# Attention's scaled gate: turned by blocks on VectorE and placed through memory

## The reference

```
attn = _sink_window_attend(q, k, v, qpos, kpos, sinks).reshape(B, T, ATTN_WIDTH)
attn = _rmsnorm(attn, attn_g) * jax.nn.silu(g_attn)
```

## Time and profile before

| | us |
|---|---|
| median of 3 runs | 2558.17 |
| the profiled execution | 2546.3 |
| its span, first to last instruction | 2544.5 |
| PE busy in the span | 2493.5 |
| VectorE busy | 1705.2 |
| ScalarE busy | 1113.5 |
| GpSimd busy | 1172.3 |

### The profile page before, as it was taken

One profiled execution on the slowest core, in us unless ns is written; L12 is line 12 of the kernel. 1 busy time (PEld: TensorE's weight loads), 2 busy tenths in 40 slices (PEclk: granted clock), 3 DMA queues, 4 the chain that ended last, 5 costly groups with the idle time before them and its releaser, 6 DMA issues. The chain is left out here.

```text
span 2544.5 us, 55195 instructions
## 1 busy us (share of the span) xinstructions
PE 2493.5 (98%) x20706; PEld 2044.3 (80%) x20706; DVE 1705.2 (67%) x3230; ACT 1113.5 (44%) x2542; POOL 1172.3 (46%) x1119
## 2 busy tenths in 40 slices
PE   8999989999999999999999999899999999999998
PEld 6788868888888788888888788688888887887887
DVE  5777777777676676654557777776777676866343
ACT  4455465555555510133334454555555554112322
POOL 2234315555556611496322443165555555116863
PEclk9999999999999999999999999999999999999999
DMA  5445552011110488765734555510111005877532
GB/s 182 154 172 185 187 186 70 27 43 43 44 38 25 175 288 293 273 216 172 264 123 154 186 179 178 190 35 31 43 43 51 31 33 195 313 270 257 170 135 91
DMA packets 176099, 365.44 MB, mean 144 GB/s; under 512 B 19104, under 2 KB 98464, under 8 KB 170272
## 3 DMA queue, kind: packets, MB, share of 16 engines
q1 hardware_dynamic: 175504, 363.11, 41.6%
q10 hardware_dynamic: 432, 0.08, 0.0%
HBM read 227.14 MB, written 137.89 MB: 143 GB/s over the span
## 5 line engine op out<-in xcount | busy, mean ns | idle before, releaser
L1947 PE MATMUL r_Z<-w_rec_parts,w_rec_xh 128*128 128x512 f32 x1920 | 610.3, 399 | 1.8 <-DVE r_kT L1768 0.9
L1947 PEld LDWEIGHTS r_Z<-w_rec_parts,w_rec_xh 128*128 128x128 f32 x1920 | 347.7, 188 | 71.9 <-issue 3.5
L1947 PE MATMUL r_Z<-w_rec_parts,w_rec_xl 128*128 128x512 f32 x960 | 375.7, 391 | 0.0
L124 PE MATMUL a_Z<-w_attn_high,w_attn_xh 128*128 128x512 f32 (+1 forms) x816 | 302.3, 370 | 11.6 <-DVE w_attn_low L211 9.7
L124 PE MATMUL a_Z<-w_attn_low,w_attn_xh 128*128 128x512 f32 (+1 forms) x816 | 290.6, 356 | 0.0
L124 PE MATMUL a_Z<-w_attn_high,w_attn_xl 128*128 128x512 f32 (+1 forms) x816 | 290.3, 356 | 0.0
L1649 ACT ACTIVATE r_E<-r_E 128x512 f32<-128x512 f32 x230 | 145.3, 632 | 294.6 <-DVE r_E L1805 292.1
L1540 POOL TENSOR_TENSOR r_qE<-r_qT,r_E 128x256 f32<-128x256 f32 x230 | 185.1, 805 | 190.6 <-ACT r_E L1649 115.4
L1947 PEld LDWEIGHTS r_Z<-w_rec_parts,w_rec_xl 128*128 128x128 f32 x960 | 180.2, 188 | 39.7
L1540 POOL TENSOR_TENSOR r_kE<-r_kT,r_E 128x256 f32<-128x256 f32 x230 | 201.2, 875 | 0.0
L124 PEld LDWEIGHTS a_Z<-w_attn_high,w_attn_xh 128*128 128x128 f32 x816 | 154.8, 190 | 39.9 <-issue 19.3
(11 more groups left out here) (338 smaller groups left out, 6409.3 us busy)
## 6 DMA issues: line engine op xcount, KB each, us to landing
dram_h_rows<-o_hb SPq DMA_DIRECT2D x34, 512.0 KB, 4.1
o_raw<-dram_hT SPq DMA_DIRECT2D x34, 512.0 KB, 4.3
o_hb<-dram_h_rows SPq DMA_DIRECT2D x34, 512.0 KB, 3.8
dram_y_all<-o_hb SPq DMA_DIRECT2D x34, 512.0 KB, 4.1
w_attn_xraw<-dram_xT SPq DMA_DIRECT2D x33, 512.0 KB, 5.7
w_rec_slot<-dram_w_in SPq DMA_DIRECT2D x16, 1024.0 KB, 8.2
o_mraw<-dram_mixT SPq DMA_DIRECT2D x32, 512.0 KB, 5.6
dram_hT<-o_hT SPq DMA_DIRECT2D x128, 128.0 KB, 2.6
```

The costliest lines, as they stand in the source:

```text
L124: mm = pe.matmul(out, a[:, c, :], b[:, c, :], start=(first and c == chunks[0] and a is xh and b is wh), stop=(last and c == chunks[-1] and ...
L1947: mm = pe.matmul(banks[what], x[:, c, :], w[:, cols[what]], start=(c == 0 and x is xh[k] and w is wh[c]), stop=(c == KC - 1 and x is xl[k]))
```

## The change

For tiles 1 to 14 the gate's transposes leave PE. VectorE turns `u` by blocks of 32x32 into `th` (`turn_gate`), right behind scale_gate, and both now stand ahead of row_max. ScalarE begins four stores of `th` into a scratch tensor in memory, which place the blocks, behind the exponentials of the same step. SyncE begins the load of the whole, now turned, into `attn`. `gated` reads `attn` in place of the PSUM bank and comes behind unfold. The values wait for the mean square of the tile before (the bank T is then free), not for `gated`. tanh, which writes `th`, waits for the load. Tiles 15 and 16 still go by PE. In the output phase semaphores are only renamed.

```
+            def load_gate_turned(j, k):
+                n = 2 * j + k
+                sp.wait_ge(*(S["turned_st0"], S["turned_st1"])[k].at(64 * (j + k)))
+                sp.wait_ge(*S["uT_out"].at(n))
+                sp.dma_start(attn[:, :], gate_home(n)).then_inc(S["turned_in"].sem, 16)
@@ SyncE, the loop; ahead of it load_gate_turned(0, 1), behind it load_gate_turned(PAIRS - 1, 0)
                 exchange_part(c)
+                load_gate_turned(j, 0)
                 store_mix(j - 1, 1)
                 load_x(j + 2, 0)
                 exchange_part(c + 1)
                 store_mix(j, 0)
                 exchange_part(c + 2)
+                load_gate_turned(j, 1)
                 if j + 2 < PAIRS:
                     load_x(j + 2, 1)
                 exchange_part(c + 3)
@@ ScalarE
+                if not isinstance(n, int) or n > 2:
+                    act.wait_ge(*S["turned_in"].at(16 * (n - 2)))
                 act.activation(th[:, :], Zg, ACT.Tanh, scale=0.5).then_inc(S["tanh_done"].sem, 1)
+            def store_gate(j, k):
+                n = 2 * j + k
+                act.wait_ge(*S["turned"].at(n))
+                for i in range(4):
+                    act.dma_start(gate_home(n).rearrange("(q r) (i x) -> i r q x", q=4, i=4)[i],
+                                 th[32 * i:32 * i + 32, :].rearrange("r (q x) -> r q x", q=4)) ...
             def rest(j, k, c=None):
                 exps(j, k)
+                store_gate(j - 1 + k, 1 - k)
                 copy_v(j + k, 1 - k)
@@ VectorE
+            def turn_gate(j, k):
+                n = 2 * j + k
+                dve.wait_ge(*S["scaled"].at(n + 1))
+                dve.transpose(th[:, :].rearrange("p (q i t) -> p q i t", q=4, i=4),
+                              u[:, :].rearrange("p (i q t) -> p q i t", q=4, i=4)).then_inc(S["turned"].sem, 1)
             def step(j, k, *chunks):
                 sum_squares(j - 1 + k, 1 - k)
+                scale_gate(j - 1 + k, 1 - k)
+                turn_gate(j - 1 + k, 1 - k)
                 row_max(j, k)
-                scale_gate(j - 1 + k, 1 - k)
...
+                unfold(j, k)
                 gated(j - 1 + k, 1 - k)
-                unfold(j, k)
@@ PE: values waits for ms_done in place of uT_out; step:
-                transpose_gate(j - 1 + k, 1 - k)
```

More of the change, by code:

```diff
@@ L70 @@
     w_split win_st x_high x_in0 x_in1 x_split y_done y_st0 y_st1 z_f z_g z_kv z_q z_v zeroed zqf_sb near_done
-    mix_st2 folded divided unfolded attnT_done summed ssq_ps gT_ps v_moved h_st0 h_st1 hT_st0 hT_st1 h_in
+    mix_st2 folded divided unfolded attnT_done summed ssq_ps gT_ps v_moved h_st0 h_st1 turned_st0 turned_st1 turned_in
     rows_in yT_st0 yT_st1 block_sum block_high block_low product c3_done recombined gate_in turned part_in0
@@ L134 @@
     **counted(NT, "x_split x_high z_kv z_q z_g rope_mul rope_sum v_copied v_moved qkT_ps qkT_sb scores_done pv_done squared"),
-    **counted(NT, "ms_done rstd_done scaled gate_done tanh_done gT_ps uT_out"),
+    **counted(NT, "ms_done rstd_done scaled gate_done tanh_done uT_out"), "gT_ps": 3, "turned": NT - 3, "turned_in": 16 * (NT - 3), "turned_st0": 64 * (PAIRS - 1), "turned_st1": 64 * (PAIRS - 1),
     **counted(NT - 1, "attnT_done summed ssq_ps"),
@@ L152 @@
     **counted(NT, "m_high m_split mix_ps summed stats_done var_done ve_done rstd_done scaled h_done"),
-    **counted(16 * NT, "m_in row_in h_in rows_in p_in"), "ln_in": 32, "weights_read": 2,
+    **counted(16 * NT, "m_in row_in turned_in rows_in p_in"), "ln_in": 32, "weights_read": 2,
     **counted(16 * (PAIRS + 1), "h_st0 y_st0"), **counted(16 * PAIRS, "h_st1 y_st1"),
-    **counted(64 * (PAIRS + 1), "hT_st0 yT_st0"), **counted(64 * PAIRS, "hT_st1 yT_st1"),
+    **counted(64 * (PAIRS + 1), "turned_st0 yT_st0"), **counted(64 * PAIRS, "turned_st1 yT_st1"),
     **counted(NT, "p_high p_split ple_ps blend y_done"), "turned": 2 * NT,
@@ L530, in attention_phase, with by_transfer @@
         own, before = slice(P, 2 * P), slice(0, P)
+        def by_transfer(n):
+            return not isinstance(n, int) or 1 <= n <= NT - 3
         part = [weights.beside[n][:, :] for n in ("part0", "part1")] + [kcT[:, :, :].rearrange("p b d -> p (b d)")]
@@ L543, in attention_phase, with gate_home @@
         upper, lower = (weights.beside[n][:, :, :].rearrange("p b d -> p (b d)") for n in ("kc", "vc"))
+        def gate_home(n):
+            return dram["hT"][layer, n][:, 0:AW]
         @block.sync
@@ L651, in _ @@
             load_x(2, 1)
+            load_gate_turned(0, 1)
             for j in range(1, PAIRS - 1):
@@ L667, in _ @@
             store_mix(PAIRS - 2, 1)
+            load_gate_turned(PAIRS - 1, 0)
             sp.wait_ge(*S["z_g"].at(NT))
@@ L911, in _ @@
             exps(PAIRS - 1, 1)
+            store_gate(PAIRS - 1, 0)
             following.round(act, lead.S, layer, 6)
@@ L1031, in scale_gate @@
                 dve.wait_ge(*S["gate_done"].at(n + 1))
-                wait(dve, S["gT_ps"], n)
+                if isinstance(n, int) and n in (1, NT - 1):
+                    dve.wait_ge(*S["gT_ps"].at(1 if n == 1 else 2))
                 dve.tensor_scalar(u[:, :].rearrange("p (i s d) -> p s i d", s=KV, d=HD),
@@ L1035, in scale_gate @@
                                   ALU.mult).then_inc(S["scaled"].sem, 1)
+            def turn_gate(j, k):
[3 more added lines that the diff above has]
+                              u[:, :].rearrange("p (i q t) -> p q i t", q=4, i=4)).then_inc(S["turned"].sem, 1)
             def gated(j, k):
                 n = 2 * j + k
-                dve.wait_ge(*S["gT_ps"].at(n + 1))
+                if by_transfer(n):
+                    dve.wait_ge(*S["turned_in"].at(16 * n))
+                    wait(dve, S["attnT_done"], n)
+                    wait(dve, (S["mix_st0"], S["mix_st1"])[k], 64 * j)
+                    dve.tensor_tensor(in_tokens(mixT[k][:, :, :]), in_tokens(attnT[:, :, :]),
+                                      attn[:, :].rearrange("p (i c t) -> p c i t", i=4, c=4), ALU.mult)                        .then_inc(S["uT_out"].sem, 1)
+                    return
+                dve.wait_ge(*S["gT_ps"].at(2 if n == NT - 2 else 3))
                 wait(dve, S["attnT_done"], n)
@@ L1239, in values @@
                 pe.wait_ge(*S["v_moved"].at(n + 1))
-                wait(pe, S["uT_out"], n)
+                if isinstance(n, int) and n in (1, NT - 1):
+                    pe.wait_ge(*S["uT_out"].at(n))
+                else:
+                    pe.wait_ge(*S["ms_done"].at(n))
                 for r in (0, 64):
@@ L2205, in output_phase @@
         K = (slice(0, KC // 2), slice(KC // 2, KC))
-        h_st, hT_st = (S["h_st0"], S["h_st1"]), (S["hT_st0"], S["hT_st1"])
+        h_st, turned_st = (S["h_st0"], S["h_st1"]), (S["turned_st0"], S["turned_st1"])
         y_st, yT_st = (S["y_st0"], S["y_st1"]), (S["yT_st0"], S["yT_st1"])
@@ L2239, in store_h @@
                 for to, of in turned_to(th[0] if n == NT - 1 else hT[k], dram["hT"][layer, n]):
-                    sp.dma_start(to, of).then_inc(hT_st[k].sem, 16)
+                    sp.dma_start(to, of).then_inc(turned_st[k].sem, 16)
             def load_h(n, made):
                 k = n % 2
-                sp.wait_ge(*hT_st[k].at(64 * (n // 2 + 1)))
+                sp.wait_ge(*turned_st[k].at(64 * (n // 2 + 1)))
                 wait(sp, S["block_low"], made)
-                sp.dma_start(raw[k][:, :, :, :].rearrange("p i c t -> p (i c t)"), dram["hT"][layer, n]).then_inc(S["h_in"].sem, 16)
+                sp.dma_start(raw[k][:, :, :, :].rearrange("p i c t -> p (i c t)"), dram["hT"][layer, n]).then_inc(S["turned_in"].sem, 16)
             def load_rows(n, came):
@@ L2350, in add @@
                 if i == 0:
-                    pool.wait_ge(*S["h_in"].at(32 * q + 32))
+                    pool.wait_ge(*S["turned_in"].at(32 * q + 32))
                     wait(pool, S["block_low"], 7 * q)
@@ L2389, in _ @@
                 low_p(0, 2 * q + 1)
-            pool.wait_ge(*S["h_in"].at(16 * NT))
+            pool.wait_ge(*S["turned_in"].at(16 * NT))
             pool.wait_ge(*S["block_low"].at(7 * PAIRS))
@@ L2413, in high @@
                 if sums[k] is None:
-                    act.wait_ge(*S["h_in"].at(16 * NT if of is not None else 32 * q + 32))
+                    act.wait_ge(*S["turned_in"].at(16 * NT if of is not None else 32 * q + 32))
                     of = (b2, a1)[k - 1] if of is None else of
@@ L2465, in _ @@
             third(0)
-            act.wait_ge(*hT_st[1].at(64 * PAIRS))
+            act.wait_ge(*turned_st[1].at(64 * PAIRS))
             high_ps(0)
@@ L2549, in turn_h @@
                 dve.wait_ge(*S["h_done"].at(n + 1))
-                wait(dve, hT_st[k], 64 * (n // 2) if isinstance(n, int) else 32 * (n - k))
+                wait(dve, turned_st[k], 64 * (n // 2) if isinstance(n, int) else 32 * (n - k))
```

(4 more changed lines are left out.)

1 line of the change is left out of this document (added).

## The result

The changed kernel takes 2625.97 us (median of 4 runs, 2622.85 to 2628.07) against 2557.66 for the kernel before beside it: ratio 1.0272, interval 1.0251 to 1.0292. The prediction said 2555, no change, and a range up to 2577. It was wrong by 71 us. The profiled execution has a span of 2621.0 us, 76.5 more than before; the medians are 68.3 apart, because the profiled execution of the kernel before was itself 11.9 us under its median.

The account below looks back on a forecast made before the run. PE, 98% busy, was taken as the bound. Gains of 12.6 and 1.7 us against 11.4 us for late gate loads gave -2.9 us: 2543.4 profiled, 2555 with the plain runs' 11.9 us offset; range 2545 to 2577.

Parts of the forecast that it names:

- row_max begins 0.5 us later: VectorE in each step: scaling (0.49 us) and turn, placed ahead of row_max, delay it and the exponentials by 0.5 us.
- the cover at the probabilities: PE comes for the probabilities 1.3 us after division ended; 0.8 us left without the transposes, hiding the late exponentials.
- PE's gain: Four gate transposes fewer per step save 0.44 us of PE in 26 steps, 11.4 us; period 18.86 us.
- The last step of each layer: The 14th step, where PE idled for unfold: unfold ahead of `gated` gains 0.6 us, 1.2 us over two layers.
- The four long steps of before: Four of 28 steps longer than 19.30 us, ascribed to late kcT landings; 1.7 us taken back as already in the new wait.
- The stores' issue: ScalarE's four gate stores begin 9.6 us after a step's start, 0.45 us per issue, and land at 13.1 us.
- The load: SyncE's load of the turned gate lands 16.9 us after step(j, 1) starts, on time; 18.75 us after step(j, 0), 0.95 late.
- the prediction's third rival: Slower: stores leave ScalarE after the exponentials or are throttled, loads land late in both kinds of step; 2574 us, chance 0.32.
- This term, +11.4: Cost of the gate's load landing 0.95 us too late for tanh in 12 steps(j, 0): 11.4 us.
- kcT "about 0.3 later": SyncE's 512 KB load of the next part into kcT, in step(j, 0), was to land about 0.3 us later.
- The place of the stall: PE was to wait for the row sums, near 1 us every second step, not before the scores or probabilities.
- The rule of the Trainium skill on one descriptor generator: SyncE's part stores would wait for up to four ScalarE issues, 1.8 us; some 20 us worse than the sum.

Follow-up runs that it names:

- e3: Kernel before, with only the gate's scaling moved ahead of row_max, no trip through memory: 2585.4 us, ratio 1.0111.
- e1: Changed kernel, with GpSimd's split_low made to wait until VectorE has done the gate's scaling: 2579.8 us, ratio 1.0092.
- e6: Changed kernel, with the gate's stores begun by SyncE right behind the turn and the load behind them, no added GpSimd wait: ratio 1.0152.
- e5: Changed kernel, with split_low waiting for the scaling and SyncE beginning the gate's stores right behind the turn, then the load: 2557.6 us, ratio 1.0002.
- e7: Changed kernel, with split_low waiting for the scaling and the gate's stores and load left out: 2549.2 us, ratio 0.9968.

## Why the prediction was wrong

The step that failed is the sentence "The scaling waits for the root, which ended at 208.05 (T+4.65); scaling 0.49, then the turn, end about T+5.9", and with it "row_max begins 0.5 us later". The 0.49 is from a row at T+9 (212.39), where GpSimd was idle. The prediction has no term for what GpSimd does at the root; in the trace of before it is this split_low:

```profile
208.01 2.39 POOL L693 TENSOR_TENSOR w_attn_xl<-w_attn_xraw,w_attn_xh 128x1024 fp32r<-128x1024 f32 x1
```

Moved up to the root, the scaling runs beside it. The term is 2.1 us larger per step, and the cover at the probabilities, put at 0.8, cannot hold it. e3 prices it alone at 28 us, e1 in the changed kernel at 46, e6 against e5 at 38. No rival named it. Hints stood in the trace of before: two of the 32 scalings, at the end of the layers and beside instructions of GpSimd, took 1324 and 1326 ns, and four low_parts took 2.00 to 2.32 us.

The other steps:
- PE's gain: right in 26 of the steps. 18.81 in e7 and e5 (said 18.86). The last step of each layer was to gain 0.6 and gained nothing: 21.12 and 21.55 in e7, 21.17 and 21.52 before.
- The cover at the probabilities: right. With the short scaling, in e1, e5 and e7, PE does not wait for them.
- The four long steps of before, from which 1.7 us was taken back: the prediction put them down to kcT's landing. It had landed at T+16.7, T+17.1, T+18.3 and T+18.7 there, and at T+17.7 and T+18.0 without a long step behind it. What all four have is the long low_part.
- The turn: 0.711 (said 0.70).
- The stores' issue runs ahead of the exponentials: right, 0.48 apart (said 0.45). But in e1 it is at T+10.2 in step(4, 0) and T+11.6 in step(4, 1), not T+9.6, and the fourth store, with the part's stores begun, lands at T+15.4 and T+16.4, not T+13.1.
- The load: in e1 at T+19.2 in step(4, 1), said T+16.9; at T+20.0 in step(4, 0), said T+18.75. So e1 is near the world of the prediction's third rival: that one said 2574 for landings of T+18.9 and T+19.2, measured 2579.8. This term, +11.4, is 32 us by e1 against e7 (1.0092 - 0.9968, of 2557). It was the second mis-sized one: without the collision the answer would still have been slower.
- kcT "about 0.3 later": 1.6 in step(4, 0) of e1 (T+19.3 and not T+17.7), and the gate's load lands behind it.
- The place of the stall: row sums every second step, as said, and beside it the probabilities, which were said to stay covered, and the values.
- The rule of the Trainium skill on one descriptor generator, locked by one sequencer at a time ("Perfetto Trace Analysis", section "Per-instruction lifecycle"), was weighed as costing 20 us. The trace of the changed kernel has both queues issuing at once in step(4, 0), and SyncE's issue of 0.38 is about as long as in the kernel before (0.37 in the median):

```profile
208.17 0.34 ACTq L882 DMA_DIRECT2D dram_hT<-a_th  x1
208.38 0.38 SPq L593 DMA_DIRECT2D dram_g_parts<-w_attn_part_high  x1
```

It is not nothing everywhere: five of ScalarE's 112 issues began while SyncE issued the load into kcT or a part (0.95 to 1.10), and took 0.71 to 1.00 in place of 0.34. How much of that is due to the lock no run shows.

The 12 us outside the steps are only in part explained. The granted clock fell to half, 1.2 GHz, in ten stretches, 44.8 us together; before it was two, 9.1 us. At half speed that is up to (44.8 - 9.1) / 2 = 18 us. Of the 44.8 us 20.9 lie outside the steps, so that at most (20.9 - 9.1) / 2 = 6 of the 12 us are the clock's. One such stretch, with what came before it (PE busy 3.64 of 5.83 us, clock in the column before the DMA share):

```profile
1455.21:1474.77 19.56, 19.02 (x140) 15.31 (x136) 15.29 (x30) 9.81 (x32) 7.32 (x6) 1.00 0.62 196
1474.77:1480.60 5.83, 3.64 (x33) 3.43 (x29) 3.44 (x4) 3.80 (x10) 2.33 (x2) 1.00 0.39 135
1480.60:1487.40 6.80, 6.50 (x42) 4.83 (x43) 5.02 (x7) 2.38 (x3) 2.86 (x2) 0.50 0.38 154
```

That PE's idling brings the fall on was not tested by itself, and e6, whose steps idle too, has only five such stretches. It stays open, as do some microseconds of the recurrence and output phases that differ from kernel to kernel.

## What to carry to other kernels

An instruction's price holds for its place. Before an SBUF-to-SBUF instruction of VectorE is moved, look at what GpSimd runs there, above all where VectorE waits for GpSimd: GpSimd's next instruction begins at that moment too. If they meet, let the long one wait, or write to PSUM. A transfer that nobody seems to wait for has a cost in its queue and in the traffic of the next: place it where the queue is empty, and take only the tiles that have such a place. Here that was worth 0.2% at most.

## What the runs showed of the hardware

- SBUF-to-SBUF scaling of 128x512: 0.49 us alone, 2.60 beside a GpSimd instruction of 2.39 that began 0.07 before it. Three times in the changed kernel VectorE began first, by 0.15 to 0.21 us: then the scaling took 0.49 and split_low 2.55 to 2.58. Once it was first by 0.01 only, and took 2.69.
- The same scaling into PSUM: 0.75, beside split_low (24 of 28) or not. VectorE's COPY_PREDICATED on the scores, which are in PSUM, ran beside split_low in the kernel before at its usual 0.70.
- `gated` took 673 to 680 ns in all 32 instances with one operand in PSUM; in 28 of them a GpSimd instruction began while it ran. With both operands in SBUF, in e5, it took 678 to 685 where GpSimd was idle, 808 once, and 1130 to 1146 (15 times) where a GpSimd instruction had begun first. So taking the operand out of PSUM cost nothing by itself, and 0.46 us beside GpSimd. How `gated` fares with one operand in PSUM where GpSimd begins first no run shows.
